# Five steps of a paged value product, each one weight chunk later in a fused decoder layer

## What is computed

```python
x = layer_norm(ALPHA * x + 0.5 * swiglu(x, ffn1...), ln_g[0], ln_b[0])
z = x @ w_in          # q, k, v | conv b, c, h | two gates
o = prompt_attention(q, k, v)                       # 256 prompt tokens
o = sample_attention(q, k_new, v_new, k_past, v_past)  # 8 sequences, 1024 past tokens each
merged = sigmoid(g_attn) * (o @ w_attn_out) + sigmoid(g_conv) * (short_conv(...) @ w_conv_out)
x = layer_norm(ALPHA * x + merged @ w_o, ln_g[1], ln_b[1])
x = layer_norm(ALPHA * x + 0.5 * swiglu(x, ffn2...), ln_g[2], ln_b[2])
```

## Time and profile before

| | |
|---|---|
| median of 3 runs | 2257.7 us (2256.88 to 2259.32) |
| the profiled execution | 2259.34 us, of which 2257.5 us are the profile's span |
| granted TensorE clock, mean over the span | 0.998 |
| PE busy | 2240.7 us, 99% |
| VectorE busy | 1366.0 us, 61% |
| ScalarE busy | 996.4 us, 44% |
| moved in all | 475.47 MB, mean 211 GB/s |

### The profile page before, as it was taken

One profiled execution on the slowest core, in us unless ns is written; L12 is line 12 of the kernel. 1 busy time (PEld: TensorE's weight loads), 2 busy tenths in 40 slices (PEclk: granted clock), 3 DMA queues, 4 the chain that ended last, 5 costly groups with the idle time before them and its releaser, 6 DMA issues.

```text
span 2257.5 us, 45691 instructions
## 1 busy us (share of the span) xinstructions
PE 2240.7 (99%) x18574; PEld 2209.3 (98%) x18574; DVE 1366.0 (61%) x1523; ACT 996.4 (44%) x1236; POOL 29.7 (1%) x59
## 2 busy tenths in 40 slices
PE   9999999999999999999999999999999999999997
PEld 9999999999999999999998899999999999999997
DVE  5545454444655689999975447896444544445554
ACT  5444444443444454454543454554444444434333
POOL 1000000000000001000000000000000000000001
PEclk9999999999999999999999999999999999999999
DMA  7656556565555688989988855556656566555553
GB/s 247 195 177 186 178 184 183 176 189 180 184 180 185 193 282 289 324 283 328 330 304 313 295 185 187 185 171 189 185 173 189 176 188 183 182 182 182 182 184 117
DMA packets 233439, 475.47 MB, mean 211 GB/s; under 512 B 18448, under 2 KB 21888, under 8 KB 233312
## 3 DMA queue, kind: packets, MB, share of 16 engines
q1 hardware_dynamic: 225920, 465.22, 63.8%
q0 software_dynamic: 2320, 5.68, 0.7%
q10 hardware_dynamic: 5072, 2.78, 0.4%
HBM read 468.13 MB, written 4.43 MB: 209 GB/s over the span
## 4 chain that ended last, share of the span: by engine, by line
PE 92%; DVE 5%; DMA 1%; issue 1%; ACT 0%; POOL 0%; DVEq 0%; ACTq 0%; POOLq 0%
PE ps L660 29%; PE ps L662 29%; PE ps L661 29%; DVE w_lo L1392 2%; PE ps L774 1%; PE ps L776 1%; PE ps L775 1%; DVE kv_ring L1724 1%; DMA w_raw<-in_w_in 1%; DVE scores L1730 1%; PE ps L917 1%; POOL y L643 0%; PE ps L863 0%; ACT w_hi L1014 0%; PE ps L805 0%
## 5 line engine op out<-in xcount | busy, mean ns | idle before, releaser
L1392 DVE TENSOR_TENSOR w_lo<-w_raw,w_hi 128x1024 fp32r<-128x1024 f32 x750 | 912.4, 1223 | 784.5 <-ACT w_hi L1014 781.6
L1014 ACT ACTIVATE w_hi<-w_raw 128x1024 fp32r<-128x1024 f32 x750 | 789.7, 1059 | 1012.1 <-PE ps L662 965.0
L660 PE MATMUL ps<-x_hi,w_hi 128*128 128x264 f32 x3840 | 1092.3, 284 | 0.5 <-ACT sig_conv L1024 0.5
L662 PE MATMUL ps<-x_hi,w_lo 128*128 128x264 f32 x3840 | 1081.5, 282 | 0.0
L661 PE MATMUL ps<-x_lo,w_hi 128*128 128x264 f32 x3840 | 1079.9, 281 | 0.0
L660 PEld LDWEIGHTS ps<-x_hi,w_hi 128*128 128x128 f32 x3840 | 720.1, 188 | 12.9 <-issue 8.6
L661 PEld LDWEIGHTS ps<-x_lo,w_hi 128*128 128x128 f32 x3840 | 723.9, 189 | 0.0
L662 PEld LDWEIGHTS ps<-x_hi,w_lo 128*128 128x128 f32 x3840 | 721.2, 188 | 0.0
L660 PE MATMUL ps<-h_hi,w_hi 128*128 128x264 f32 x1408 | 398.0, 283 | 0.0
L661 PE MATMUL ps<-h_lo,w_hi 128*128 128x264 f32 x1408 | 397.7, 282 | 0.0
L662 PE MATMUL ps<-h_hi,w_lo 128*128 128x264 f32 x1408 | 397.5, 282 | 0.0
(11 more groups left out here) (268 smaller groups left out, 1370.8 us busy)
## 6 DMA issues: line engine op xcount, KB each, us to landing
w_raw<-in_ffn_w_down SPq DMA_DIRECT2D x176, 512.0 KB, 3.8
w_raw<-in_ffn_w_gate SPq DMA_DIRECT2D x175, 512.0 KB, 3.7
w_raw<-in_ffn_w_up SPq DMA_DIRECT2D x175, 512.0 KB, 3.8
w_raw<-in_w_in SPq DMA_DIRECT2D x160, 512.0 KB, 5.0
kv_ring<-in_cache_k SPq DMA_DIRECT2D x64, 512.0 KB, 6.0
kv_ring<-in_cache_v SPq DMA_DIRECT2D x64, 512.0 KB, 6.3
w_raw<-in_w_o SPq DMA_DIRECT2D x32, 512.0 KB, 4.3
w_raw<-in_w_conv_out SPq DMA_DIRECT2D x16, 512.0 KB, 4.9
```

The source lines that it names most:

```text
L660: nc.tensor.matmul(acc, wh, hi[:, kt], start=(kt == 0), stop=False)
L662: return nc.tensor.matmul(acc, wl, hi[:, kt], start=False, stop=last)
L1014: nc.scalar.activation(w_hi[:, s], w_raw[:, s], ACT.Copy).then_inc(w_hi_ready, 1)
L1392: V.tensor_tensor(w_lo[:, s], w_raw[:, s], w_hi[:, s].bitcast(F32), ALU.subtract).then_inc(w_lo_ready, 1)
```

## The change

The first five entries of `V_STEP` become 73, 79, 89, 95 and 101; the other eleven stay. The list is read by PE's `middle`, by the plan of the page loads (`PAGE_ORDER`, `PAGE_LOAD`, and with them each page's slot) and by `SUMS_OUT` and `BY_HEAD`, which take entries that stay.

```diff
         SOFTMAX_BANKS = (7, 6), (4, 5)
         NEW_TOKEN = 12, 10
-        V_STEP = 72, 78, 88, 94, 100, 107, 113, 120, 123, 127, 131, 134, 137, 140, 144, 147
+        V_STEP = 73, 79, 89, 95, 101, 107, 113, 120, 123, 127, 131, 134, 137, 140, 144, 147
         SUMS_OUT = [V_STEP[PAGES * (g + 1) - 1] for g in range(GROUPS)]
         BY_HEAD = V_STEP[-1] + 3
         HEAD = 38, 50, 62, 78, 88, 122, 131, 140
```

## The result

The changed kernel takes 2262.28 us (median of 18 runs, 2259.75 to 2265.68), the kernel before 2257.84 (18 runs beside it): ratio 1.0016, interval 1.001 to 1.0023. It is slower by 4.4 us. That is under the 0.2% which the prediction took as the least that counts, but clear of noise, on the other side of the forecast, and outside its range of 2254.4 to 2259.9. Two executions, of 12,071 us (one of d3) and 4,487 us (one of the kernel before, run beside d1 to d4), were in a slow state and stand in no ratio.

The account below looks back on a forecast made before the run. PE, busy 99%, bounds the kernel, so only its waits count: -0.8 + 0.9 + 0.4 - 0.3 - 0.7 = -0.5, taken as -0.6 from 2259.34; less 1.6 for the profiled run, 2257.1 us. Range 2254.4 to 2259.9.

Parts of the forecast that it names:

- Step 0: Step moved from chunk 72 to 73: its 0.76 us wait for o_new goes, a gain of 0.8 us.
- Step 1: Chunk 78 to 79: last page lands later, wait 1.3 to 2.9 us instead of 0.95; loss taken as 0.9.
- Seams: The second and third moved steps now stand alone: 0.2 us more for each, 0.4 together.
- Step 2: Chunk 88 to 89: no wait before, none after, with 1 us in hand for its last page.
- Step 3: Chunk 94 to 95: page wait shrinks to 0.4 us (-0.3); chunk 96's wait for its bank goes (-0.7).
- Step 4 and later: Chunk 100 to 101: no wait, margin of about 1.4 us stays; from the sixth step, over 4 us in hand.
- R1: All waits go: 3.1 us less 0.4 for seams, 2255.0 us; chance 0.10.
- R2: Pages of the step at chunk 95 land 2.4 us later than forecast: +1.6, 2259.3 us; chance 0.22.
- R3: Weights starve from chunk 83 on, PE waiting chunk by chunk for w_lo: +5 to +8 us, 2264; chance 0.04.
- R4: Nothing at all: the waits only move, 2257.7 us; chance 0.04.

Follow-up runs that it names:

- d3: Changed kernel with SP's page numbers loaded ahead and ScalarE's two convolution-state stores 14 chunks later: 2258.91 us, ratio 1.0003.
- d1: Kernel before, unchanged, run again for a second trace: the traced execution took 2259.36 us.
- d4: Kernel before with SP's page numbers loaded ahead and ScalarE's two convolution-state stores 14 chunks later: 2257.66 us, ratio 0.9999.
- b3: Changed kernel with nine matmuls on constants added ahead of step 1 to fill some 2 us of its wait: 2261.57 us, ratio 1.0017.
- f2: Changed kernel, but in the page-load plan only step 2's entry is new (89), the others as before: 2261.42 us, ratio 1.0012.
- f1: Changed kernel, but in the page-load plan only the entries 95 and 101 are new, the others as before: 2259.13 us, ratio 1.0008.
- a3: Changed kernel with step 0 back at chunk 72, the other four steps moved: 2261.85 us, ratio 1.0018.
- d2: Changed kernel, unchanged, run again for a second trace: the traced execution took 2262.11 us.
- a4: Changed kernel's step places, but page loads in the order and chunks of the kernel before: 2258.23 us, ratio 1.0002.
- e3: Kernel before with only ScalarE's two convolution-state stores moved 14 chunks later, to chunk 102: 2258.13 us, ratio 1.0000.
- a1: Kernel before with only step 1 moved, from chunk 78 to 79: 2260.04 us, ratio 1.0009.
- b2: Changed kernel with ScalarE's two convolution-state stores issued 14 chunks later, at 102 instead of 88: 2261.14 us, ratio 1.0016.
- e1: Changed kernel with step 0 back at chunk 72 and ScalarE's two convolution-state stores moved to chunk 102: 2261.19 us, ratio 1.0012.
- c1: Changed kernel, but the page-load plan takes old entries 72 and 78, then new ones 89, 95 and 101: 2262.14 us, ratio 1.0018.
- a2: Kernel before's step places, but page loads in the order and chunks of the changed kernel: 2272.35 us, ratio 1.0061.
- b1: Changed kernel, but SP loads each group's page numbers right after the page ahead of it in the order: 2259.23 us, ratio 1.0006.

## Why the prediction was wrong

*What bounds the kernel*: right. The traces' loss is all in PE's stretch from 1037 to 1125, and hardly any of it shows in the shares of the page.

*Step 0*: right (-0.83 for -0.8), in both traces of the changed kernel.

*Step 1*: the price of this term failed. Its mechanism was right in each part: weights first, uncovered page numbers, fifth page at 1062.2 to 1063.8 (measured 1063.3), a wait of 1.3 to 2.9 us (2.68; 3.33 in the second trace). Two things were wrong in the sum. I took 0.9 for the loss, "nearer the low end", where the wait alone lost 1.7 and the bound said up to 1.9. And the price of a wait was put at its length. The granted clock halved as PE started again, for 3.4 us, another 1.7 (b3). The term was 3.4 us instead of 0.9, and that alone brings the forecast of 2257.1 to about 2259.6.

*Seams*: right for step 2 (+0.20).

*Step 2*: this step failed in its mechanism. "No wait, with 1 us in hand" looked at the pages, and for them it held. It didn't ask what else was behind the delayed transfers: ScalarE rounds chunk 90 ahead of emptying chunk 88's bank. The prediction had found this very link for chunks 96 and 98 and did not apply it to the panel before. It cost 1.98 us in one trace and 0 in the other; plans that differ in the entries of steps 2 to 4, step 2's new in one, differ by 2.3 in the median (f2 against f1). Why the load of chunk 90's weights takes longer in some executions stays open.

*Step 3*: by its own sum right: -1.22 against -1.0; chunk 96's wait gone, the page's wait 0.19. But "this page's time does not depend on PE, so step 3 acts as a meeting point" was wrong. The page landed at 1119.9, not 1115.6. In a3, d2 and the first trace PE reached step 3 2.65, 3.9 and 4.6 us behind the kernel before, SP issued this page at 1110.5, 1111.8 and 1112.5, and PE's wait ended at 1118.0, 1119.3 and 1119.95: 7.5 us after the issue each time, and later by as much as PE was. By the kernel's text SP waits for VectorE, VectorE for ScalarE and ScalarE for PE's release of the slots. Nothing was made good there.

*Step 4 and later*: right (+0.03, then nothing).

*The rivals*: R1, all waits go, is what a4 was meant to be, and it failed as well: PE's earlier arrival is met by VectorE at chunk 84 and by the bank at 96. The gains that were forecast had a ceiling that the rows of one trace do not show: the 0.95 us of step 1 were 0.27 in d1 and 0.17 in e3, whose edit comes later, and step 3's 0.65 were 0.38 and nothing; R1 deserved less than its 0.10 and the forecast less than 0.60. R2 named the right sign for the wrong place. R3's mechanism did not occur: no weight matmul waited for w_lo.

The Trainium skill's rule "Overlap DMA with compute" ("DMA: Bandwidth & Descriptors", Rules for kernel authors), to issue early and wait late, points the right way: undoing the later issue and keeping the later wait (a4) takes the loss away, and buys nothing. As R4 priced it, no change at all, it missed as well. The 358 GB/s of the Trainium skill ("DMA: Bandwidth & Descriptors", Specifications) is half of a memory stack's 716, for two cores. This kernel, on one core, moved 397 to 409 GB/s in four windows of 2 to 4 us, and 313 over the 103 us of the stretch.

Open: the traces give +2.4 and +3.7 us for the stretch, the medians +4.4. The two traced executions of the kernel before took 1.5 and 1.1 us more than the medians beside them. Where other executions save this is only hinted at: e3's traced one is at the median and takes 1.6 us less for the stretch, as it hardly waits at steps 1 and 3. And the losses of a1 and a3 in the medians, 2.2 and 4.0 us, are explained by their traces only in part.

## What to carry to other kernels

Ask of a moved step which computed times hang on it: here moving one consumer by a chunk moved the next consumer's transfers by a chunk too, past register loads that had been hidden. Price a wait of TensorE of two to three microseconds at more than its length, since here the clock mostly halved with it. And when a transfer becomes later, follow the engine that waits for it through everything that is queued behind it there, above all the emptying of a PSUM bank.

## What the runs showed of the hardware

- The granted clock fell to 0.5 with idle times of PE of 2.68 (changed kernel), 3.33 (d2), 2.80 (b2), 2.10 (e1), 2.08 (f2), 2.68 (c1), 3.42 and 2.08 us (a2), for 3.4 us or, in c1 and at a2's first, 6.8. It did not with 0.77 (b1), 1.75 (changed kernel) and 1.80 (b3), nor with one of 2.60 (a2, ahead of step 2). The fall came 0.2 to 0.9 us after PE had started again in five of the eight, and 0.7 to 1.5 us before that in b2, c1 and a2's first, so part of it then lay in the idle time. With 0.5 us idle and 2.3 us of small fp32 matmuls in the same gap (b3) it stayed at 1.00.
- Loading eight page numbers into SP's registers holds SP up: 2.8 us lie between the weights and the burst in the changed kernel, and with the loads ahead (b1) the burst starts 2.4 us earlier. That is about five page transfers' worth of issuing (0.5 us each).
- Two stores with 70 KB in some 2,080 packets on ScalarE's queue slow what else is moved: from 1083 to 1092 us the DMA engines moved 189 to 247 GB/s in the 12 traces that have the stores there, and 300 to 376 in the 6 that have them later.
